# Where a hybrid conv/pool/PEER layer splits its weights and activations: pooled products read earlier, norm results split on the vector engine, three weight splits moved

## The reference

```python
def rmsnorm(x, g):
    xf = x.astype(jnp.float32)
    y = xf * lax.rsqrt(jnp.mean(xf * xf, axis=-1, keepdims=True) + EPS)
    return (y * g.astype(jnp.float32)).astype(x.dtype)
...
def mix_even(h, prev_a, prev_b, pos0, w_in, dw_a, db_a, ln_g, ln_b, w_pool, pool_scale, w_out):
    p = h @ w_in
    a_lin, a_gate, b_in = p[..., :D_A], p[..., D_A:2 * D_A], p[..., 2 * D_A:]
    a = a_lin * jax.nn.sigmoid(a_gate)
    ext_a = jnp.concatenate([prev_a, a], axis=1)
    a_conv = depthwise_causal_conv(ext_a, dw_a) + db_a
    a_out = jax.nn.silu(layernorm(a_conv, ln_g, ln_b))
    ext_b = jnp.concatenate([prev_b, b_in], axis=1)
    pooled = (multiscale_pool(ext_b, pos0, t) - b_in).reshape(bsz, t, N_POOL_GROUPS, D_POOL_GROUP)
    b_out = jnp.einsum('btgc,gcd->btgd', pooled, w_pool).reshape(bsz, t, D_B) * pool_scale
    y = jnp.concatenate([a_out, b_out], axis=-1) @ w_out
...
    c_act = jax.nn.silu(c)
    for l in range(DEPTH):
        mod = c_act @ w_ada[l] + b_ada[l]
        sh1, sc1, g1, sh2, sc2, g2 = [mm[:, None, :] for mm in jnp.split(mod, N_MOD, axis=-1)]
        h = rmsnorm(x, norm_mix_g[l]) * (1 + sc1) + sh1
        ...
        x = x + g1 * y
        h = rmsnorm(x, norm_ffn_g[l]) * (1 + sc2) + sh2
        x = x + g2 * peer(h, peer_wq[l], peer_k1[l], peer_k2[l], peer_u[l], peer_v[l])
    return rmsnorm(x, final_g), jnp.stack(new_a), jnp.stack(new_b), jnp.stack(new_c)
```

## Time and profile before

| | us |
|---|---|
| median of three executions (3771.55 to 3772.61) | 3772.31 |
| the profiled execution, its whole time | 3770.65 |
| its span, as the profile shows it | 3768.9 |
| PE busy in the span | 3627.0 (96%) |
| DVE busy | 2586.1 (69%) |
| ACT busy | 1027.2 (27%) |

### The profile page before, as it was taken

How to read it: one execution, slowest core, us unless ns; L and a number is a source line. 1 busy time by engine, 2 the same in 40 slices (tenths; PEclk the granted TensorE clock), 3 DMA queues, 4 the chain that set the end, 5 groups by cost and what they waited for, 6 DMA issues and landing times.

```text
span 3768.9 us, 72843 instructions
## 1 busy us (share of the span) xinstructions
PE 3627.0 (96%) x31816; PEld 2959.8 (79%) x31816; DVE 2586.1 (69%) x3938; ACT 1027.2 (27%) x922; POOL 11.9 (0%) x34
## 2 busy tenths in 40 slices
PE   7778999999999999999979899999999999999998
PEld 3357888888888888888845688888888888888886
DVE  4857755556665888888734585555666488888886
ACT  3034333343332111111132333243343411111111
POOL 0000000000000000000000000000000000000000
PEclk9889999999999999999989999999999999999999
DMA  8732245454558454545312213464554775454540
GB/s 339 315 119 76 92 160 193 172 194 174 190 203 312 184 195 192 198 184 197 135 67 90 103 68 137 161 203 158 195 197 167 247 278 198 184 195 187 203 184 35
DMA packets 196225, 667.12 MB, mean 177 GB/s; under 512 B 11952, under 2 KB 151360, under 8 KB 152512
## 3 DMA queue, kind: packets, MB, share of 16 engines
q1 hardware_dynamic: 190608, 663.67, 47.3%
q10 hardware_dynamic: 5392, 0.56, 0.1%
q0 software_dynamic: 32, 0.01, 0.0%
HBM read 514.72 MB, written 149.49 MB: 176 GB/s over the span
## 4 chain that ended last, share of the span: by engine, by line
PE 92%; DVE 4%; DMA 3%; ACT 1%; issue 0%; SPq 0%; DVEq 0%; ACTq 0%
PE PS L732 38%; PE PS L688 35%; PE PS L663 5%; PE PS L600 4%; PE PS L718 3%; PE PS L580 2%; PE PS L613 1%; PE PS L627 1%; DMA ring<-whole_w 1%; DMA arena<-gates_dram 1%; PE PS L676 1%; ACT H L856 1%; DVE ring L1193 1%; PE PS L595 1%; DMA arena<-act_dram 1%; DVE arena L1307 1%
## 5 line engine op out<-in xcount | busy, mean ns | idle before, releaser
L688 PE MATMUL PS<-X,ring 128*128 128x272 f16 x12288 | 1437.0, 279 | 0.0
L732 PE MATMUL PS<-arena,ring 128*128 128x272 f16 x12288 | 1423.7, 279 | 2.6 <-DVE ring L1193 2.6
L732 PEld LDWEIGHTS PS<-arena,ring 128*128 128x128 f16 x12288 | 1202.2, 98 | 224.1 <-issue 3.2
L688 PEld LDWEIGHTS PS<-X,ring 128*128 128x128 f16 x12288 | 1198.8, 98 | 218.7 <-issue 0.4
L1193 DVE SCALAR_TENSOR_TENSOR ring<-ring 128x4096 f16<-128x4096 f32 x149 | 659.0, 4424 | 637.5 <-ACT ring L865 628.9
L865 ACT ACTIVATE ring<-ring 128x4096 f16<-128x4096 f32 x149 | 538.5, 3615 | 1154.8 <-PE PS L732 1119.3
L1539 DVE TENSOR_TENSOR ACC<-PS,ACC 128x544 f32<-128x544 f32 x512 | 363.1, 719 | 236.0 <-PE PS L732 236.0
L1035 ACT ACTIVATE H<-PS 128x544 f32<-128x544 f32 x256 | 159.7, 624 | 974.6 <-PE PS L688 974.5
L1529 DVE TENSOR_TENSOR arena<-arena 128x544 f32<-128x544 f32 x256 | 292.6, 1143 | 45.7 <-DMA arena<-act_dram 45.7
L663 PE MATMUL PS<-X,ring 128*128 128x272 f16 x1536 | 186.4, 282 | 29.4 <-DVE X L1200 29.4
L663 PEld LDWEIGHTS PS<-X,ring 128*128 128x128 f16 x1536 | 149.4, 99 | 63.5 <-issue 35.1
(11 more groups left out here) (149 smaller groups left out, 1538.1 us busy)
## 6 DMA issues: line engine op xcount, KB each, us to landing
ring<-U SPq DMA_DIRECT2D x64, 2048.0 KB, 10.6
ring<-V SPq DMA_DIRECT2D x64, 2048.0 KB, 7.6
act_dram<-H SPq DMA_DIRECT2D x64, 1088.0 KB, 5.0
gates_dram<-ACC SPq DMA_DIRECT2D x68, 1024.0 KB, 5.7
arena<-gates_dram SPq DMA_DIRECT2D x32, 2176.0 KB, 9.5
arena<-act_dram SPq DMA_DIRECT2D x64, 1088.0 KB, 5.0
ring<-split_w SPq DMA_DIRECT2D x17, 2048.0 KB, 9.0
arena<-whole_w SPq DMA_DIRECT2D x11, 2048.0 KB, 10.9
```

What stands on the lines that cost most here:

```text
L688: mm = pe.matmul(ps_halves(u)[:, half, :], parts[lane][:, pu, k * 512 + j * P:k * 512 + (j + 1) * P], H16[:, ph, k, half * HALF:(half + 1) ...
L732: mm = pe.matmul(ps_halves(u)[:, half, :], parts[lane][:, pv, j * D + c * P:j * D + (c + 1) * P], WT[:, grp, pw, j, half * HALF:(half + 1) ...
```

## The change

- **Pooled products.** PE makes three pooled products ahead of modulation slot 20, and the fourth after slots 20 and 21 with a turn between them. DVE reads the first three after tap 15 (`i == 14`), the fourth after tap 20 (`i == 19`); the low part of the output weights' first slot comes after tap 23 (`i == 22`). ACT writes its high part right after the fourth pooled copy, ahead of the last modulation rows.
- **Norm results.** In the three norms where ACT wrote the high parts of H, DVE now writes both halves, chunk by chunk (`split_part`), as soon as `modulate` has done a chunk. That is 24 casts that move from ACT to DVE. In the feedforward norms the wait for `x_stored` (X is overwritten by the halves) moves along to DVE.
- **Second query slot** (lane 1, both layers). ACT splits it between the squares and the root, DVE ahead of reading the sum.
- **Layer 1's first two slots.** The first is split in the last V product of layer 0: ACT as soon as the product before it is done, DVE after the third of the eight adds. The second is split after the norm: ACT behind `modulate`, DVE behind the split of H.

```diff
@@ tensor @@
-                    for g in range(KA):
+                    for g in range(KA - 1):
                         pool_branch(g)
-                    for s in range(20, 2 * ADA_SLOTS):
-                        ada_rows(s)
-                        if s % 4 == 0:
-                            ada_turn(s // 4 - 1)
-                    ada_turn(2 * ADA_SLOTS // 4 - 1)
+                    ada_rows(20)
+                    ada_turn(4)
+                    ada_rows(21)
+                    pool_branch(KA - 1)
+                    ada_rows(22)
+                    ada_rows(23)
+                    ada_turn(5)
@@ scalar @@
                 else:
                     squares(X, H, KD, x_ready, 1)
-                    for lane in range(2):
-                        high(lane, U_SCALE)
                     root()
                     modulate(l, 0)
-                    high_part(H, HM[l], h_ready, 2 * KD * l + 1, hm_high)
+                    high(1, U_SCALE)
...
-                    for g in range(KA):
+                    for g in range(KA - 1):
                         take_pool(g)
                     take_turn(4)
+                    take_pool(KA - 1)
+                    high(0, 1.0)
                     take_rows(5)
-                    high(0, 1.0)
                     take_turn(5)
                     high(1, 1.0)
...
                         act.activation(H[:, k, :], X[:, k, :], ACT.Square).then_inc(sq_ready, 1)
+                high(1, U_SCALE)
                 root()
                 modulate(l, 1)
-                act.wait_ge(x_stored, 16 * (l + 1))
-                high_part(H, H16, h_ready, 2 * KD * l + KD + 1, h_high)
-                high(1, U_SCALE)
...
                         w.take("dve", KD)
+                if l + 1 < LAYERS:
+                    high(0, U_SCALE)
                 w.take("dve", KD)
@@ vector @@
-            def low_part(src, dst, signal_high, signal):
+            def split_part(src, dst, made, signal_high, signal):
                 for k in range(KD):
+                    dve.wait_ge(h_ready, made + k + 1)
+                    dve.tensor_copy(dst[:, 0, k, :], src[:, k, :]).then_inc(signal_high, 1)
                     dve.wait_ge(signal_high, l * KD + k + 1)
                     dve.tensor_tensor(dst[:, 1, k, :], src[:, k, :], dst[:, 0, k, :], ALU.subtract).then_inc(signal, 1)
...
                 else:
-                    for lane in range(2):
-                        low(lane, U_SCALE)
                     norm_x(4)
-                    low_part(H, HM[l], hm_high, hm_split)
-                    for lane in (0, 1, 0, 1):
+                    split_part(H, HM[l], 2 * KD * l, hm_high, hm_split)
+                    for lane in (1, 0, 1, 0, 1):
                         low(lane, U_SCALE)
...
-                            if first == 2 and i == 24:
-                                for g in range(KA):
+                            if first == 2 and i in (14, 19):
+                                for g in range(KA - 1) if i == 14 else (KA - 1,):
...
+                            if first == 2 and i == 22:
                                 low(0, 1.0)
...
                 residual(l, "g1", False)
+                low(1, U_SCALE)
                 norm_x((3, 5)[l])
-                low_part(H, H16, h_high, h_split)
-                low(1, U_SCALE)
+                dve.wait_ge(x_stored, 16 * (l + 1))
+                split_part(H, H16, 2 * KD * l + KD, h_high, h_split)
...
+                        if not more and l + 1 < LAYERS and c == 2:
+                            low(0, U_SCALE)
```

10 lines of the change are left out of this document (1 added, 9 removed).

## The result

The changed kernel takes 3735.1 us (median of four, 3733.9 to 3737.0) against 3771.9 (3771.3 to 3772.6) for the kernel before, read beside it: 0.990 of the time, interval 0.989 to 0.992. The prediction was 3733.0, range 3730.5 to 3741.5. The profiled execution took 3734.5; its span is 3732.3, where it was 3768.9: 36.6 us less against 39.3 forecast.

The account below looks back on a forecast made before the run. PE, busy in 96% of the 3768.9 us span, was taken as the bound, so only its waits count. Gains 24.6 + 11.1 + 3.6 = 39.3 us take the median from 3772.3 to 3733.0, range 3730.5 to 3741.5.

Parts of the forecast that it names:

- Rival 1: Clock stays at half until PE's first chunk is whole, in three places: +2.2 us, 3735.2; chance 0.08.
- Part A: Layer 0's pooled products: reordering ends the layer-norm sums at 192.7 instead of 217.35, -24.6 us; bounds -25.0 and -20.
- The ring of waits: Layer 0: PE waits for DVE's late reads, ACT for PE's late modulation slots, DVE 20.77 us for ACT's weight slot.
- both conditions of PE's output projection fall at 179.5 to 179.8: Layer 0: DVE's low part and the last modulation turn both ready then, where it was 205.0; PE starts about 179.9.
- Landings: Layer 0 modulation transfers after issue: slots 21 and 22 taken to land after 7.7 us, slot 23 after 9.5.
- rival 2: Modulation slots set layer 0: landings stretch to 11.8 us, pooled part gives 20, total 3737.6; chance 0.10.
- Part B: Layer 1's entry: sum read at once, H split on DVE in 1.11 us pairs; first chunk read earlier, -11.1 us.
- Part C: Two feedforward norms: first query chunk read at 300.55 instead of 302.36, -1.8 us each, -3.6 in all.
- the query slot ahead of the norm: Feedforward norms: DVE's low part delays the read of the sum, an added wait of 1.1 us.
- Those for the entry and the norms: Signs: entry read 0.1 us after sums, PE wait some 11, chunk after 19.3; norms read 1.1 late, wait about 12.
- The first read of the layer-norm sums: Sign for layer 0: DVE's first read of these sums comes 24 to 25 us earlier.
- DMA waits of L627 over 10 us: Sign that would show the forecast wrong: PE's modulation slots waiting that long for their transfers.

Follow-up runs that it names:

- experiment 1: Changed kernel with the pooled products and weight slot back in the old order on PE, ACT and DVE: 3754.7 us, 19.6 above the changed kernel.
- experiment 11: Changed kernel with query low part behind H's split, H's casts shared by DVE and ACT, unread matmuls filling PE's gaps (modulation slots, norms, sums): 3743.9 us.
- Experiment 9: Changed kernel with ACT making all high parts of H again at layer 1's entry, weight slots left where the change put them: 3736.8 us (+1.7).
- experiment 4: Changed kernel with layer 1's entry undone, both weight slots ahead of the norm and H's high parts on ACT: 3743.1 us (+8.0).
- Experiment 6: Changed kernel with only the second query slot's low part moved back behind the split of H on DVE, both layers: 3730.6 us (-4.5).

## Why the prediction held, and where it was off

**The forecast: right in kind, 2.1 us short in the median** (3735.1 for 3733.0), inside the range. At the entry and in both feedforward norms the chain that ended last was the one forecast, at its price. In layer 0 it was not: PE ended last, which the forecast had under a microsecond behind DVE's taps. That the median came so near is in part luck, since the stretch in layer 0 alone varies by 3.4 us from profile to profile. Rival 1's 3735.2 is met to 0.1 by chance as well; its mechanism is ruled out below.

**Part A, -24.6 forecast, -23.3 in the trace** (22 by experiment 1, 20.6 to 24.0 over eight profiles). The ring of waits went as described: no wait of L646 for DVE, and one wait of DVE of 0.81. The step that failed is "both conditions of PE's output projection fall at 179.5 to 179.8". DVE's fell at 181.4 (1.1 of it from the slower first sums, 0.8 from the wait), PE's own chain of modulation slots only at 183.5. The terms of that chain, one by one:
- Landings. From its issue to the matmuls that waited for it, slot 21 took 8.8 us (issued at 157.53), not 7.7; slot 22 took 9.9 (162.74), not 7.7; slot 23 took 8.3 (169.24), less than its 9.5. The rows of before had 7.7 and 9.5 in one place and 11.8 in another, and I had taken the best one twice. The three issues in the timeline:

```profile
157.53 0.35 SPq L404 DMA_DIRECT2D arena<-whole_w  x1
162.74 0.33 SPq L404 DMA_DIRECT2D H<-whole_w  x1
169.24 0.35 SPq L404 DMA_DIRECT2D arena<-whole_w  x1
```

- Slot 21 ran partly at half clock: 2.83 us where 1.92 is the full one. With its issue 1.0 later and its transfer 1.1 longer than forecast, that made slot 23's issue three microseconds late. The fourth product took 2.01 where 1.27 is the full one; it is not in this chain, but delayed DVE by the 0.81.
- Slot 23's rows took 3.56 us, not 1.9. The granted clock over them was 0.52, in the window that follows (us; busy time and count of PE, PEld, DVE, ACT, POOL; clock; DMA share; GB/s). I had the price of half clock for PE's first product in each norm, but not for a slot of 16 matmuls behind a wait of 3.02. The prediction contradicts itself here: it says that PE starts at half clock after every gap, and takes 1.9 from the row of rows 4 in which a slot behind a wait of 1.56 ran at full clock.

```profile
177.60:181.00 3.40, 3.40 (x16) 0.55 (x16) 3.40 (x1) 0.00 (x0) 0.00 (x0) 0.52 0.00 0
```

The slot began 1.9 us after the forecast's 175.7, and its rows added 1.6: that is nearly all of the 3.6 by which PE was late. Little of it reached the end. DVE's taps ended at 193.0; with one chunk of sums behind them, 1.1, they would have set the end at 194.1, and PE set it at 195.2. In this profile Part A thus lost 1.3, of which 1.0 is PE's chain; in four of the eight it is 3.3 to 3.6. This is rival 2 by its link (the slots set layer 0), but less by its cause, landings of 11.8, than by the half clock: experiment 11, with the clock kept up, gets the full 24.6. Rival 2's own price was also mis-added. With 11.8 for slots 21 and 23, its chain ends 4.1 + 2.3 = 6.4 us later and not about 4, which leaves some 17.6 of Part A and not 20.

**Part B, -11.1 forecast, -11.0 measured.** The chunk was read 19.45 us after the sums against 19.3, and the pieces are the forecast's: the read 0.1 after the sums, pairs of 1.11, PE 0.2 behind. The low part in the last V product delayed one of the eight adds, and PE had no wait there: its row in the timeline runs on through DVE's 4.42 from 1859.64. (The 2.9 us that V's products wait in all are for weight slots, before 2.6.)

```profile
1844.83 27.96 PE L732 MATMUL PS<-arena,ring 128*128 128x272 f16 x240
```

Experiment 9 splits the term in 3.9 for the split of H and 7.1 for the slots; in experiment 4 the slots show only 6.0, because PE's first product there ran more at full clock.

**Part C, -1.8 each forecast, -1.74 measured.** Experiment 6 confirms the term inside it: the query slot ahead of the norm costs 1.0 (forecast +1.1) and could be had back.

**The signs named beforehand.** Those for the entry and the norms came as written. The first read of the layer-norm sums came 22.2 us earlier (217.46 to 195.28) and not 24 to 25. "DMA waits of L627 over 10 us" was to mean that the forecast is wrong: the row in the page is 12.9, but 7.2 of it is one wait ahead of the pooled products, 7.0 before; the waits for slots 21 to 23 are 7.2 together, before 6.3.

**The clock while PE is fed in pieces.** Rival 1 had it stay at half until the first chunk was whole. One of the windows of the changed kernel at the entry, while the last pieces come (columns as above), has it at full:

```profile
1901.00:1902.00 1.00, 0.78 (x7) 0.35 (x6) 0.96 (x3) 0.08 (x1) 0.00 (x0) 1.00 0.00 0
```

In the first feedforward norm it is 1.00 as well from 275.4 to 277.4. So the rival is out. The Trainium skill, "TensorE: Matmul & The Clock Gate", section "HAM oscillation — how this bites in real kernels", describes a kernel whose TensorE waits for a transfer after each short burst of matmuls and starts every burst at the low clock. This trace agrees where PE waited 3.02 us for slot 23 (clock 0.52 over its rows). Pieces 0.2 us apart are not the case that the section describes, and here the clock came back between them.

**What no step had: the scatter of the sums.** The sums at the entry and of the last norm come 2.7 us after V's last product. The trace of the changed kernel has 8.81 us for the one and 11.81 for the other, the same instructions after the same gap. The windows of the first half of each (columns as above) show the clock at 1.00 and at 0.50:

```profile
1875.50:1880.00 4.50, 4.50 (x17) 2.59 (x18) 4.50 (x11) 3.64 (x6) 0.00 (x0) 1.00 0.01 2
3707.60:3712.00 4.40, 4.40 (x9) 2.33 (x9) 4.40 (x11) 3.56 (x6) 0.00 (x0) 0.50 0.01 2
```

Over the profiles of all kernels these sums took 8.7 to 8.8, 10.5 or 11.8 to 11.9 us, with no relation to the edit: the changed kernel's own second profile has 10.50 and 10.49. What decides it is not shown. In the twelve profiles without filler ahead of them, the two together took 17.6 us three times, 20.6 to 20.7 three times and 21.0 six times. So they move a time by up to 3.4 us, beside the 3.4 of layer 0. The very first sums varied too, 10.4 to 11.8; the clock column reads 1.00 there throughout, so what slows them stays open.
